# Modulation beside the wide block: VectorE adds up the weight tiles times silu(c), TensorE only adds over the partitions once per vector group

## The reference, cut to what matters

```python
ml = (jax.nn.silu(c) @ ada_w[l] + ada_b[l]).reshape(B, N_MOD, 1, D)
mc = (jax.nn.silu(c_ctx) @ ada_w[l] + ada_b[l]).reshape(N_MOD, 1, 1, D)
x = x + 0.5 * ml[:, 2] * _swiglu(_modulate(_rms(x, ffn1_norm[l]), ml[:, 0], ml[:, 1]), ffn1_w_in[l], ffn1_w_out[l])
h = h + 0.5 * mc[2] * _swiglu(_modulate(_rms(h, ffn1_norm[l]), mc[0], mc[1]), ffn1_w_in[l], ffn1_w_out[l])
```

## Time and profile before

| | us |
|---|---|
| median of 3 runs | 2444.39 |
| lowest, highest | 2444.21, 2450.21 |
| the profiled execution, its time | 2452.57 |
| its span | 2450.8 |
| TensorE, VectorE, ScalarE busy in it | 2385.1, 1434.5, 1120.3 |
| the wide up pass: first matmul to the SiLU of tile 21 | 40.87 to 320.18 |

### The profile page before, as it was taken

How to read it: one execution, slowest core, us unless ns; L and a number is a source line. 1 busy time by engine, 2 the same in 40 slices (tenths; PEclk the granted TensorE clock), 3 DMA queues, 4 the chain that set the end, 5 groups by cost and what they waited for, 6 DMA issues and landing times.

```text
span 2450.8 us, 33208 instructions
## 1 busy us (share of the span) xinstructions
PE 2385.1 (97%) x13574; PEld 1989.7 (81%) x13574; DVE 1434.5 (59%) x2114; ACT 1120.3 (46%) x1686; POOL 13.1 (1%) x43
## 2 busy tenths in 40 slices
PE   7999999999999999999999999999999999999998
PEld 4776788888888887888788888888888888787887
DVE  3222232745747487666766568666666665776665
ACT  4212232524632425544544467554454445764444
POOL 0000000000000000000000000000000000000000
PEclk9999999999999999999999999999999999999999
DMA  8565222313441223555555554345545555434553
GB/s 325 232 237 189 86 100 90 132 60 120 154 153 70 87 87 138 181 189 189 198 189 189 201 187 153 141 158 188 190 172 189 191 181 217 144 142 159 189 189 138
DMA packets 57910, 399.65 MB, mean 163 GB/s; under 512 B 7785, under 2 KB 8305, under 8 KB 10272
## 3 DMA queue, kind: packets, MB, share of 16 engines
q1 hardware_dynamic: 52704, 383.80, 43.0%
q10 hardware_dynamic: 4264, 10.07, 1.2%
q0 software_dynamic: 800, 3.73, 0.5%
HBM read 396.52 MB, written 2.63 MB: 163 GB/s over the span
## 4 chain that ended last, share of the span: by engine, by line
PE 90%; DVE 4%; ACT 3%; DMA 2%; issue 1%; SPq 0%; DVEq 0%; ACTq 0%
PE pair L477 84%; DMA ring<-in_stream 2%; PE pair L808 1%; PE pair L586 1%; DVE ring_parts L2072 1%; PE pair L791 1%; PE pair L944 1%; PE pair L603 1%; ACT mix_high L1437 0%; ACT arena L1777 0%; ACT arena L1387 0%; ACT xT L1415 0%; PE pair L755 0%; PE pair L1222 0%; DVE rows L2167 0%
## 5 line engine op out<-in xcount | busy, mean ns | idle before, releaser
L477 PE MATMUL pair<-xT_parts,ring_high 128*128 128x512 f32 x2112 | 745.6, 395 | 3.6 <-DVE xT_parts L2054 3.6
L477 PE MATMUL pair<-xT_parts,ring_parts 128*128 128x256 f32 (+2 forms) x2448 | 693.1, 298 | 4.0 <-DVE ring_parts L2072 1.8
L2062 DVE TENSOR_TENSOR ring_parts<-ring,ring_high 128x2048 fp32r<-128x2048 f32 x198 | 453.5, 2292 | 159.4 <-ACT ring_high L1424 159.3
L477 PEld LDWEIGHTS pair<-xT_parts,ring_parts 128*128 128x128 f32 (+1 forms) x2448 | 460.0, 188 | 52.9 <-issue 18.2
L477 PEld LDWEIGHTS pair<-xT_parts,ring_high 128*128 128x128 f32 x2112 | 383.9, 188 | 79.8 <-issue 4.4
L1424 ACT ACTIVATE ring_high<-ring 128x2048 fp32r<-128x2048 f32 x198 | 378.2, 1911 | 97.3 <-DMA ring<-in_stream 97.1
L2072 DVE TENSOR_TENSOR ring_parts<-ring,mix_high 128x1024 fp32r<-128x1024 f32 x144 | 168.4, 1219 | 77.6 <-ACT mix_high L1437 77.3
L1469 ACT ACTIVATE arena<-pair 128x512 f32<-128x512 f32 x110 | 66.0, 600 | 309.3 <-PE pair L477 309.3
L1437 ACT ACTIVATE mix_high<-ring 128x1024 fp32r<-128x1024 f32 x144 | 142.9, 1049 | 98.7 <-DMA ring<-in_stream 96.6
L477 PE MATMUL pair<-ring_parts,xT_parts 128*128 128x512 f32 (+1 forms) x448 | 176.6, 394 | 2.6 <-ACT arena L1753 2.4
L477 PE MATMUL pair<-mix_high,xT_parts 128*128 128x512 f32 (+1 forms) x576 | 172.5, 383 | 0.0
(11 more groups left out here) (389 smaller groups left out, 3786.4 us busy)
## 6 DMA issues: line engine op xcount, KB each, us to landing
ring<-in_stream SPq DMA_DIRECT2D x338, 1024.0 KB, 4.8
xn<-in_mods SPq DMA_DIRECT2D x14, 1024.0 KB, 7.0
arena<-in_mods SPq DMA_DIRECT2D x14, 1024.0 KB, 9.2
arena<-in_bT ACTq DMA_DIRECT2D x1, 1536.0 KB, 10.3
bias_scratch<-bias_row POOLq DMA_DIRECT2D x1, 1536.0 KB, 8.2
X<-in_x ACTq DMA_DIRECT2D x1, 1024.0 KB, 11.9
X<-in_ctx ACTq DMA_DIRECT2D x1, 1024.0 KB, 16.4
arena<-in_bT ACTq DMA_DIRECT2D x1, 1024.0 KB, 8.5
```

What stands on the lines that cost most here:

```text
L477: m = pe.matmul(o, l, r, start=start, stop=stop)
L2062: dve.tensor_tensor(out=ring_r[:, slot].rearrange("p a b -> p (a b)"), in0=w, in1=high[:, slot, :], op=ALU.subtract).then_inc(low_ready, 1)
```

## The change

TensorE no longer multiplies groups 1 to 4. VectorE multiplies each 128 x 2048 chunk, partition by partition, with silu(c) as a column (`cT`, on which ACT now also takes SiLU in place), and adds it up over the slices into SBUF tiles (`sums_of`): 2048 columns of multiply-adds per chunk for groups 2 and 4, 3072 for group 3, 4096 for group 1, because the context row is needed in full for group 1 and for half of group 3. When a group is whole, TensorE adds over the 128 partitions with a matrix of ones in one column (`summing`), a few matmuls per group (`quad_sums`): groups 3, 4 and 2 behind tile 9, group 1 behind tile 15. The order of the chunks is new: groups 3, 2 and 4 interleaved in tiles 0 to 7 (two chunks in even steps, three in odd ones, `MOD_STEPS`), none in step 8, then group 1 in steps 9 to 13. The buffers are now freed by VectorE's `modulation_steps`. The rows of group 2 are turned behind tile 11 and those of group 1 behind tile 17. The sums lie in parts of `arena` that later products of the block overwrite, so DVE waits for TensorE's sums in step 9 and before product 15.

```diff
-MOD_TILES = 14
+MOD_ROWS = {0: 1, 3: 2, 4: 3, 2: 4, 1: 5}
+MOD_KEPT = {0: 1, 2: 2, 1: 3}
+MOD_BANK = {0: 4, 3: 5, 4: 4, 2: 7, 1: 5}
+MOD_ORDER = [m for k in range(8) for m in ((3, k), (2, k), *(((4, k // 2),) if k % 2 else ()))] + \
+            [(1, k) for k in range(8)]
+MOD_STEPS = [2 + f % 2 for f in range(8)] + [0, 2, 2, 1, 2, 1]
+MOD_TILES = len(MOD_STEPS)
...
+        summing = ones[:, 0:64].rearrange("p (r c) -> p r c", c=32)
+        low_sums, high_sums = room(FT * 2 * S, 2 * N), room(25 * 1024, 2 * N)
+        sums_of = {3: [[room(14 * N, 4 * N)], [low_sums]], 4: [[high_sums]], 2: [[room(10 * N, 4 * N)]],
+                   1: [[room(15 * N, 3 * N), tmp[:, 1, :]], [low_sums, high_sums]]}
+        turned_row = {0: modrow[:, 0, :], 3: modrow[:, 1, :], 4: modrow[:, 0, :], 2: room(13 * N, N),
+                      1: room(20 * N, N)}
+        mod_parts = {q: 2 if q == 4 else 1 for q in sums_of}
+        mod_per = {q: mod_parts[q] * sum(len(rooms) for rooms in sums_of[q]) for q in sums_of}
+        mod_after = list(itertools.accumulate(mod_per[q] for q, k in MOD_ORDER))
+        mod_summed = {q: max(mod_after[n] for n, m in enumerate(MOD_ORDER) if m[0] == q) for q in sums_of}
...
                 f = n - QUAD - 3
                 if 0 <= f < MOD_TILES:
-                    for s in range(2):
-                        if f:
-                            sp.wait_ge(mod_read[s], f)
-                        sp.dma_start(mod_w[s], t["mods"][2 * f + s]).then_inc(mod_loaded[s], 16)
+                    for m in range(sum(MOD_STEPS[:f]), sum(MOD_STEPS[:f + 1])):
+                        if m >= 2:
+                            sp.wait_ge(mod_step, mod_after[m - 2])
+                        sp.dma_start(mod_w[m % 2], t["mods"][m]).then_inc(mod_loaded[m % 2], 16)
...
+            def quad_sums(q):
+
+                pe.wait_ge(ones_set, 1)
+                pe.wait_ge(mod_step, mod_summed[q])
+                if q == 1:
+                    pe.wait_ge(mod_row, MOD_ROWS[3])
+                rooms = sums_of[q]
+                groups = [[v[:, at:at + N] for v in row for at in range(0, v.shape[-1], N)] for row in rooms]
+                for r, row in enumerate(groups):
+                    for g, v in enumerate(row):
+                        last = r == len(groups) - 1
+                        mm(bank[MOD_BANK[q]][32 * g:32 * g + 32, :], summing[:, r, :], v, r == 0,
+                           g >= len(groups[-1]) or last, mod_full if last and g == len(row) - 1 else None)
             def quad_turn(q):
...
-                pe.wait_ge(mod_row, q + 1)
+                pe.wait_ge(mod_row, MOD_ROWS[q])
                 if q:
-                    pe.wait_ge(mod_kept, q)
+                    pe.wait_ge(mod_kept, MOD_KEPT[q] - 1)
...
             def gate_row(n):
...
                 if n == 0:
-                    pe.wait_ge(mod_kept, 3)
+                    pe.wait_ge(mod_kept, MOD_KEPT[2])
...
             def beside_up(f):
 
-                for s in range(2 if f < MOD_TILES else 0):
-                    n = 2 * f + s
-                    q, k = 1 + n // KD, n % KD
-                    if k == 0 and q >= 2:
-                        pe.wait_ge(mod_row, q - 1)
-                    pe.wait_ge(mod_loaded[s], 16 * (f + 1))
-                    if q < 4:
-                        quad_part(q, k, mod_w[s], mod_full if k == KD - 1 else None)
-                    else:
-                        quad_part(q, 2 * k, mod_w[s])
-                        quad_part(q, 2 * k + 1, mod_w[s][:, 2:4, :], mod_full if 2 * k + 1 == KD - 1 else None)
-                    owed.append(mod_read[s])
-                if f in (5, 9):
-                    quad_turn((f - 1) // 4)
+                for q in {9: (3, 4, 2), 15: (1,)}.get(f, ()):
+                    quad_sums(q)
+                if f in (11, 17):
+                    quad_turn(2 if f == 11 else 1)
                 if f in (13, 15, 17, 19):
                     gate_row(f - 13)
                     gate_row(f - 12)
...
                 act.activation(scT[:, :, 0:2], cT[:, :, :], ACT.Silu).then_inc(sc_done, 1)
+                act.wait_ge(sc_done, 1)
+                act.activation(cT[:, :, :], cT[:, :, :], ACT.Silu).then_inc(sc_done, 1)
...
+                for at, end, value in ((0, 1, 1.0), (1, 33, 0.0), (33, 34, 1.0), (34, 64, 0.0)):
+                    ins = dve.memset(ones[:, at:end], value)
+                ins.then_inc(ones_set, 1)
+
+            def mod_products(m):
+
+                dve.wait_ge(mod_loaded[m % 2], 16 * (m // 2 + 1))
+                if m == 0:
+                    dve.wait_ge(sc_done, 2)
+                q, k_ = MOD_ORDER[m]
+                if k_:
+                    dve.wait_ge(mod_step, mod_after[MOD_ORDER.index((q, k_ - 1))])
+                for half in range(mod_parts[q]):
+                    k = mod_parts[q] * k_ + half
+                    if half:
+                        dve.wait_ge(mod_step, mod_after[m] - 1)
+                    for r, rooms in enumerate(sums_of[q]):
+                        at = half * 2 * N
+                        for total in rooms:
+                            w = mod_w[m % 2].rearrange("p a b -> p (a b)")[:, at:at + total.shape[-1]]
+                            at += total.shape[-1]
+                            if k == 0:
+                                ins = dve.tensor_scalar(total, w, cT[:, k, r:r + 1], None, ALU.mult)
+                            else:
+                                ins = dve.scalar_tensor_tensor(out=total, in0=w, scalar=cT[:, k, r:r + 1], in1=total,
+                                                               op0=ALU.mult, op1=ALU.add)
+                            ins.then_inc(mod_step, 1)
...
-                if f in (4, 8, 12):
-                    quad_row(f // 4)
-                if f in (6, 10):
-                    quad_keep((f - 2) // 4)
-                if f == 14:
-                    quad_row(4)
+                if f == 9:
+                    dve.wait_ge(mod_full, MOD_ROWS[2])
+                for m in range(sum(MOD_STEPS[:f]), sum(MOD_STEPS[:f + 1])):
+                    mod_products(m)
+                for q in {10: (3, 4, 2), 16: (1,)}.get(f, ()):
+                    quad_row(q)
+                if f in (12, 18):
+                    quad_keep(2 if f == 12 else 1)
...
                 def product_wide(f):
 
+                    if f == 15:
+                        dve.wait_ge(mod_full, MOD_ROWS[1])
                     dve.wait_ge(sil4_done, f + 1)
```

More of the change, by code:

```diff
@@ L1 @@
+import itertools
 import math
@@ L281, in build @@
         mod_loaded = [sem(f"modulation_chunk_loaded{i}") for i in range(2)]
-        mod_read = [sem(f"modulation_chunk_read{i}") for i in range(2)]
+        mod_step = sem("modulation_steps")
         mod_full = sem("modulation_products")
@@ L515, in group_tile, with quad_part @@
                     owed.append(read[(ch + 1) % SLOTS])
-            def quad_part(q, k, w, inc=None):
-                groups = 2 * len(MODS[q])
-                for g in range(groups):
-                    mm(bank[4 + q % 2][32 * g:32 * g + 32, :], scT[:, k, :], w[:, g, :], k == 0, k == KD - 1,
-                       inc if g == groups - 1 else None)
+            def quad_part(k, w, inc=None):
+                for g in range(4):
+                    mm(bank[4][32 * g:32 * g + 32, :], scT[:, k, :], w[:, g, :], k == 0, k == KD - 1,
+                       inc if g == 3 else None)
+            def quad_sums(q):
[10 more added lines that the diff above has]
+                           g >= len(groups[-1]) or last, mod_full if last and g == len(row) - 1 else None)
             def quad_turn(q):
-                pe.wait_ge(mod_row, q + 1)
+                pe.wait_ge(mod_row, MOD_ROWS[q])
                 if q:
-                    pe.wait_ge(mod_kept, q)
+                    pe.wait_ge(mod_kept, MOD_KEPT[q] - 1)
                 picked = ident[:, :].rearrange("p (a b) -> p a b", b=32)[:, :, 0:2]
                 for j in range(4):
-                    mm(bank[6][:, 8 * j:8 * j + 8], modrow[:, q % 2, j * P:(j + 1) * P], picked, True, True,
-                       mod_turned if j == 3 else None)
+                    mm(bank[4 if q == 1 else 6][:, 8 * j:8 * j + 8], turned_row[q][:, j * P:(j + 1) * P], picked,
+                       True, True, mod_turned if j == 3 else None)
             def gate_row(n):
                 q, g, r = GATE_ROWS[n][:3]
-                pe.wait_ge(mod_row, q + 1)
+                pe.wait_ge(mod_row, MOD_ROWS[q])
                 if n == 0:
-                    pe.wait_ge(mod_kept, 3)
+                    pe.wait_ge(mod_kept, MOD_KEPT[2])
                     pe.wait_ge(late_consts, LATE_CONSTS)
@@ L543, in gate_row @@
                 rows_ = slice(32 * g, 32 * g + 2)
-                mm(bank[6 + n % 2][:, :], pick[rows_, r, :], modrow[rows_, q % 2, :], True, True, bc_full)
+                mm(bank[6 + n % 2][:, :], pick[rows_, r, :], turned_row[q][rows_, :], True, True, bc_full)
```

(13 more changed lines are left out.)

4 lines of the change are left out of this document (2 added, 2 removed).

## The result

| | before | after |
|---|---|---|
| median of 5 runs, us | 2444.39 | 2434.02 |
| lowest, highest | 2443.22, 2452.19 | 2433.46, 2435.71 |
| profiled execution: time, span | 2452.57, 2450.8 | 2434.63, 2432.9 |
| T_0 to T_21 in it | 268.11 | 255.99 |

The ratio to the kernel before, from the runs of one chip, is 0.9946 with a 95% interval of 0.9931 to 0.9962: 0.4 to 0.7% faster, or some 13 us of 2444 (9 to 17 by the interval). The medians lie 10.4 us apart.

What follows compares the result with a forecast made beforehand. TensorE, 97% busy, was taken to bound the kernel. 32.8 - 6.1 - 0.6 - 5.5 - 3.8 - 3.2 = 13.6 us won, taking the median from 2444.4 to 2431; eight in ten: 2421 to 2440.

Steps and rivals of the forecast that it cites:

- T_0: ScalarE's SiLU of tile 0 in the wide up pass, 52.07 us before the change; T_f is that of tile f.
- products removed: Wide up pass: all 112 modulation matmuls of the stage leave TensorE, 32.8 us less.
- sums on TensorE: Behind tiles 9 and 15: 20 new matmuls over the summed tiles cost TensorE 6.1 us.
- wait 1, the lag: Up to tile 8: VectorE falls behind as third chunks and ring loads hold each other up; TensorE waits 0.6 us.
- wait 2, the turn: Behind tile 11: TensorE's turn waits for bias rows VectorE makes behind two chunks of group 1; 5.5 us.
- wait 3, gate row 0: Behind tile 13: gate row 0 waits for group 2's keep, behind two chunks of group 1; 3.8 us.
- clock: Behind tiles 11 and 13: the granted clock falls after the two long waits; 3.2 us, bounds 0 and 5.
- won in the stage: Wide up pass: matmuls removed, less sums, three waits and lower clock, 13.6 us won.
- its limit of T_5 + 21.1: Up to tile 8: VectorE may end at T_f + 21.1, as TensorE needs tile f+1's product when tile f+3 starts.
- The full gain: Rival: the waits behind tiles 11 and 13 don't bind, adds costing little over half the price; 2418 to 2424, chance 0.1.
- The other two: Rivals: transfer circle slower or adds 1.15 times, 2437 to 2450, chance 0.2; VectorE bounds tiles 1 to 13, slower, chance 0.05.
- near 90% busy: Sign: VectorE busy near 90% from 60 to 210 us.

Runs made afterwards that it cites:

- experiment 5: Changed kernel with bias rows and group 2's keep ahead of the chunks, and SP issuing third chunks behind the next ring load; 2416.42 us, ratio 0.9868.
- experiment 1: Changed kernel with step 10's bias rows and step 12's keep of group 2 put ahead of the chunks on VectorE; 2422.70 us, ratio 0.9892.
- experiment 2: Changed kernel with only the bias rows of step 10 put ahead of the chunks; 2425.11 us, ratio 0.9905.
- experiment 3: Changed kernel with only the keep of group 2 put ahead of step 12's chunks; 2431.47 us, ratio 0.9925.
- experiment 4: Changed kernel with the keep first and the bias rows between the two chunks of step 10; 2422.11 us, ratio 0.9885.
- experiment 9: The changed kernel as it is, run once more; 2432.82 us, ratio 0.9950 to the kernel before.
- experiment 7: Kernel of experiment 5 with step 10's bias rows behind the first operation of that step's second chunk; 2425.84 us, ratio 0.9924.
- experiment 8: Kernel of experiment 5 with step 10's bias rows behind three of four operations of that step's second chunk; 2428.33 us, ratio 0.9930.
- experiment 10: Kernel of experiment 5 run once more, on the same chip as experiment 9; 2418.36 us, ratio 0.9884.

## Why the prediction was right

Forecast 2431, measured 2434.0, or -13.2 us by the ratio where -13.6 was forecast. The mechanism was right: what was removed, what came, both waits and where they stand, and the falls of the clock behind them. That the whole came so near is in part luck: in the stage 12.1 us were won and not 13.6, and scatter outside it made up the rest. By its terms, in the profiled execution:

| term | predicted | measured |
|---|---|---|
| products removed | 32.8 | 32.8 (experiment 5) |
| sums on TensorE | 6.1 | 5.6 |
| wait 1, the lag | 0.6 | 0.1 (0.5 to 1.6 in experiments 1 to 4 and 9) |
| wait 2, the turn | 5.5 | 5.5 |
| wait 3, gate row 0 | 3.8 | 3.8 |
| clock | 3.2 | 5.6 (6.4 in experiment 9) |
| won in the stage | 13.6 | 12.1 |

- The waits came out to a tenth because they were worked out as moments on two engines: third row done at T_10 + 16.3 (forecast 16.3), keep done at T_12 + 14.6 (14.7). The adds kept to their prices, which are pitches: an add of 1536 begins at 169.31 and the next operation at 171.04, 1.73 for a forecast 1.72 (its duration is 1.81), and two chunks of group 1 take from 169.31 to 179.08, 9.77 for 9.8.
- The mis-sized term is the clock: 3.2 for 5.6. The prediction took 1.6 us a fall from two stretches of the kernel before. Cut into pieces of 2 us, the first of them reads:

```profile
444.00:446.00 2.00, 1.94 (x10) 1.65 (x10) 1.88 (x5) 0.66 (x2) 0.00 (x0) 0.77 0.33 55
446.00:448.00 2.00, 2.00 (x12) 2.00 (x11) 1.97 (x3) 1.31 (x4) 0.00 (x0) 0.50 1.04 432
448.00:450.00 2.00, 2.00 (x18) 2.00 (x18) 1.40 (x4) 1.51 (x4) 0.00 (x0) 0.88 0.74 299
```

That is 3.4 us of work at the lower level, with TensorE as busy as in the tiles. The assumption that failed is that every fall lasts so long: behind wait 3 of the changed kernel it did (3.4 us, 1.7 lost), behind wait 2 TensorE worked 7.8 us at 1.2 GHz, and between 5.8 and 6.8 in experiments 2, 3 and 9. Experiments 1 to 3 show that the falls belong to the waits; why they last 3.4 us in one place and twice that in another is open.
- Wait 1: third chunks done at T_1 + 16.8, T_3 + 19.2 and T_5 + 20.8 (forecast 17.45, 19.5, 21.6), 23.5 from pair to pair rather than 23.9. At tile 5 VectorE was thus 0.3 inside its limit of T_5 + 21.1 in the changed kernel, and 0.6 over it in experiment 1 (T_5 + 21.7, from 126.08 + 2.61 - 106.98), where TensorE waited 0.7. Such tenths decide between no wait and one of 1.3 us (experiment 3). In the changed kernel's profile T_6 to T_8 is 21.82 for 21.76; tile 7's own SiLU stands 0.7 late there (128.89), which ScalarE gives back by tile 8, so a SiLU marks the end of a tile only where ScalarE isn't late itself.
- The rest is scatter outside the stage. From T_21 to the end the profiles take 2130.6 us before, 2124.9 after, 2126.3 in experiment 9, and 2122.0 to 2133.7 in the others, in code that no edit touches. The profiled execution of before lay 8.2 us over the median, that of after 0.6; hence 17.9 us between the two spans for 12.1 in the stage. The granted clock goes with it: of eleven executions of the kernel before beside experiments 7 to 10, the one at a mean of 0.990 took 2453.1 us and the two at 0.997 took 2444.2 and 2444.6. Why the clock differs from one execution to the next is open.
- Two rules were weighed in the prediction. The Trainium skill, VectorE: DVE Perf Modes, "The DRAIN you can't avoid", says that the next operation does not start until the pipeline is empty, and that one that isn't held starts earlier. The changed kernel's adds of 2048 and 1024 take 3.55 us together where alone they are 2.35 and 1.28: they overlap by 0.08 us, so the full duration of each, as the prediction read the rule, is too much here too. The Trainium skill, DMA: Bandwidth & Descriptors, "Where 436 GB/s comes from", puts the limit of a core's reading from HBM at some 358 GB/s. The changed kernel moved 413 GB/s from 150 to 160 us, with one core at work; 358 isn't the limit here.
- The full gain was the rival to which the kernel could be brought (2416 to 2418), but not by cheaper adds, as it supposed: by their place in the list. The other two fall: the pair of tiles took 23.5 us and not 26.1, and no add cost 1.15 times its price.
- One sign missed: VectorE was to be near 90% busy from 60 to 210 us and is busy 117.84 of these 150, or 79% (84% in experiment 1). The other signs were there: 10.88 from SiLU to SiLU in tiles 1 to 6, 40 records on `ones`, the waits of 5.49 and 3.85, adds of 2.35 us, a lower clock at 179 to 189 and 213 to 216, and 2.3 to 2.6 us of waiting for a third chunk.
